# Woven attention: unscaled probabilities, and an output scaled by rows of inverses that pass through memory

## The chip, the cores and the metric

One Trainium2 chip, one of its cores. The metric is the time of one execution in device microseconds (us); smaller is better. The kernel before took 2072.51 us, the median of 3 runs (2071.71 to 2074.53).

## The reference, cut to what matters

A stack of layers on 512 tokens of width 1024, in float32. Three of the layers hold an attention, each followed by an output projection. Two have sinks (a window attention, a chunk band attention), the third has a bias from a table. In all three a softmax is divided by its row sum before it is multiplied with the values:

```python
m = jnp.maximum(jnp.max(scores, axis=-1, keepdims=True), sink_l)
p = jnp.exp(scores - m)
denom = jnp.sum(p, axis=-1, keepdims=True) + jnp.exp(sink_l - m)
p = (p / denom).astype(v.dtype)
out = jnp.einsum('bnkgqs,bnskd->bnqkgd', p, vb)
...
else:
    p = jax.nn.softmax(s, axis=-1)
o = jnp.einsum('bhgqj,bjhd->bqhgd', p.astype(v.dtype), v_c)
```

## The kernel before

Activations lie transposed: features on the 128 partitions, the 512 tokens in the free dimension. A weight matrix comes from memory in pairs of tiles (`raw`). ScalarE (ACT) rounds a piece to `w_hi` (L1621), VectorE (DVE) subtracts to get the rest `w_lo` (L1629), and TensorE (PE) makes each product of three matmuls of 128x512 (L1184 to L1186): hi by hi, hi by lo, lo by hi. One such triple is a *step*. The activations are split in the same way; for the attention's output the two halves are `mix_hi` and `mix_lo`, which the trace calls `act`.

An attention is woven into the steps of the projections around it: in1/out1 and in2/out2 (the grouped attentions, a = 0 and 1) and in3/out3 (the wide one). The work is cut into *slots*, and a table of step numbers (`GSLOTS`, `SLOTS`) says after which step each engine does its part of slot i. All engines run their instructions strictly in the order of the program, with semaphores between them. Two heads make a *chunk* c; there are 4 in a grouped attention and 8 in the wide one. A chunk has 4 blocks of 128 queries in 3 parts, one part to a slot: the unit u. A slot works on several units at once:

- PE, slot i: the scores of unit i (L504 wide, L666 grouped), the transposes of the probabilities of unit i-2 (L651, grouped alone), and the weighted sums of values of an older unit (L517, L684) into a bank of the accumulator (`pair_bank(c)`).
- DVE, slot i: for unit i-1 the inverse of the row sums (L572, L726) and the scaling of the probabilities, one instruction for each block and head (L576, L730); in the wide attention then a copy that splits each word in two halves (`halves`, L583); for unit i the biased maxima (L593, L740). After the last unit of a chunk the rest `mix_lo` (L599, L747).
- ACT, slot i: the exponentials of unit i with their row sums (L561, L715), the copy of the transposed unit out of the accumulator or out of `crossed` (L704, L549), and `mix_hi` of a finished chunk straight from the accumulator (L555, L708).
- SP, the queue that issues transfers: in the wide attention a transposing transfer of `halves` to `crossed` for each unit (L527); in the grouped ones the shifted rows of the rotary embedding (L760, L761) and the loads of weights (L1105).

Other DVE work stands between the slots in the same queue: `ring` (L2341, queries and keys of the wide attention, which PE's scores of a chunk wait for), `proj` (L2272) and the rotary embedding (L776 to L781) of the grouped ones, and the results of the output projection (`h` L2309, `y` L2305 and L2355). Fourteen steps before the end of in1 and in2 PE transposes the values (L1485); it waits there for the tile that L2272 writes.

The output projection takes chunks 4 to 7 in its first 32 steps in out1 and out2 (made by the pooling and by the recurrence) and the attention's own 0 to 3 after them, out3 the chunks 0 to 3 and then 4 to 7; out1's step 36 is the first that reads chunk 3 of the attention. DVE's slot 15, which ends that chunk, stands at step 35 of out1 and at step 32 of out2.

Of the kernel before, what the change touches and what calls it, by code (L numbers as in the profile page):

```python
# [5 lines left out]
F32 = mybir.dt.float32  # L6
# [6 lines left out]
P = 128  # L13
# [155 lines left out]
def build(nc, x_t, vecs, weights, mixer_consts, pool_tab, small_consts, pool_w, sinks, rel_bias, out_t, scratch, skew, stop=None):  # L169
# [4 lines left out]
    with ExitStack() as ctx:  # L174
# [51 lines left out]
        mask = mconst[:, 2 * T:2 * T + 384]  # L226
        squares = at("squares", [P, KD * T], F32, act_at)
# [103 lines left out]
        w_normed = sem("w_normed")  # L331
# [17 lines left out]
        g_normed = sem("g_normed")  # L349
# [32 lines left out]
        std4, inv4 = tiny[:, 112:116], tiny[:, 116:120]  # L382
        sink_col, neg_sink, decay = tiny[:, 80:96], tiny[:, 96:112], tiny[:, 128:192]
# [105 lines left out]
        def slot_pe(pe, i):  # L489
# [31 lines left out]
        def slot_sp(sp, u):  # L521
# [17 lines left out]
        def slot_act(eng, i):  # L539
# [12 lines left out]
            c, s = divmod(i - 7, NPARTS)  # L552
            if s == 0 and 0 <= c < KD:
                eng.wait_ge(w_weighed, NPARTS * (c + 1))
                eng.activation(chunk(mix_hi, c), pair_bank(c), ACT.Copy).then_inc(w_mix_hi, 1)  # L555
            if 0 <= i < STEPS:
                c, s, own, _ = blocks_of(i)
                for part, (n, at_, w) in enumerate(own):
                    for hh in range(2):
# [3 lines left out]
                                       accum_out=ROW[:, part_col(i, part, hh)]).then_inc(w_probs, 1)  # L563

        def slot_dve(eng, i, link):

            u = i - 1
            if 0 <= u < STEPS:
# [14 lines left out]
                eng.tensor_copy(to, words).then_inc(w_halved, 1)  # L583
            if 0 <= i < STEPS:
# [53 lines left out]
        def grouped_pe(pe, a, i):  # L638
# [31 lines left out]
            for u in (i - 4, i - 3) if i % 2 == 0 else ():  # L670
# [4 lines left out]
                if s == 0:  # L675
                    pe.wait_ge(g_v_done, a + 1)
                    if c >= 2:
                        pe.wait_ge(mix_ready, KD * a + 4 + c - 1)
# [15 lines left out]
        def grouped_act(eng, a, i):  # L694
# [10 lines left out]
            c = mixed_at(a, i)  # L705
            if c is not None:
                eng.wait_ge(g_weighed, u0 + len(GPARTS[a]) * (c + 1))
                eng.activation(chunk(mix_hi, c), pair_bank(c), ACT.Copy).then_inc(mix_hi_ready, 1)  # L708
            if 0 <= i < GSTEPS[a]:
                c, s, own, _ = grouped_blocks(a, i)  # L710
                for part, (n, lo, hi, at_, w) in enumerate(own):
                    for hh in range(2):
# [3 lines left out]
                                       accum_out=ROW[:, grouped_col(i, part, hh)]).then_inc(g_exped, 1)  # L716

        def grouped_dve(eng, a, i, link):
# [3 lines left out]
            if 0 <= u < GSTEPS[a]:  # L722
# [3 lines left out]
                link(eng.reciprocal(INV[:, grouped_col(u, n=rows)], ROW[:, grouped_col(u, n=rows)]))  # L726
                for part, (n, lo, hi, at_, w) in enumerate(own):
                    for hh in range(2):
                        p = exps_at(a, u, hh)[:, at_:at_ + w]
                        ins = eng.tensor_scalar(p, p, INV[:, grouped_col(u, part, hh)], None, ALU.mult)  # L730
# [344 lines left out]
        def _(sp):  # L1075
            for st in stages:
# [30 lines left out]
                if st.name in IN:  # L1107
                    a = IN.index(st.name)
                    out = OUTS[a]
                    for g in range(-2 * KD * 2, 2 * KD * (st.pairs + out.pairs - 2)):  # L1110
# [6 lines left out]
                        if g % KD == 1 and g // KD - 1 in ROPED[a]:  # L1117
                            rope_sp(sp, a, g // KD - 1)
# [1505 lines left out]
```

## Time and profile before

| what | value |
|---|---|
| median of 3 runs | 2072.51 us |
| the profiled execution | 2075.14 us, of which its span is 2073.3 us |
| granted clock of TensorE, mean | 0.999 |
| busy, share of the span: PE, DVE, ACT | 99%, 57%, 37% |

The span is the time from the first to the last instruction of the program in the profile; 1.8 us of the execution lie around it. PE is the engine that everything else must keep fed. Its matmuls overlap and their ends are modelled, so that lost time shows best in the distance of one matmul's start to the next: in a step it is 0.23 us.

### The profile page before, as it was taken

How to read it: one execution, taken by the hardware profiler on the slowest of the kernel's cores; microseconds unless marked ns; L12 is line 12 of the kernel's file. 1: busy time of each engine (PE TensorE's matmuls, PEld its weight loads, DVE VectorE, ACT ScalarE, POOL GpSimd, SP SyncE). 2: the span in 40 equal slices, each digit the busy share in tenths (PEclk: the TensorE clock that was granted, in tenths of full speed). 3: DMA queues.
4: the chain of work that ended last, by engine and by line, in shares of the span. 5: the costliest groups of instructions: out<-in, count | busy, mean ns of one | idle time of the engine just before them, and what ended most of it. 6: DMA issues, size and time to landing. Idle time of an engine off the chain costs nothing.

```text
span 2073.3 us, 27109 instructions
## 1 busy us (share of the span) xinstructions
PE 2055.2 (99%) x10366; PEld 1689.7 (81%) x10366; DVE 1180.8 (57%) x1927; ACT 759.5 (37%) x1163; POOL 123.8 (6%) x138
## 2 busy tenths in 40 slices
PE   9999999999999999999999999999999999999999
PEld 7888888778888888988788888888876688888887
DVE  5444433786444433487778666633668877666433
ACT  5222222354322222463454322222557753222222
POOL 0000000400000000000002000000413120000001
PEclk9999999999999999999999999999999999999999
DMA  8322233312222222331221322233347622232222
GB/s 255 121 98 101 76 99 108 130 47 96 86 101 101 96 69 98 116 102 62 92 82 62 101 101 101 76 99 109 103 128 166 158 78 102 101 101 95 72 96 82
DMA packets 78300, 210.90 MB, mean 102 GB/s; under 512 B 46192, under 2 KB 49568, under 8 KB 61840
## 3 DMA queue, kind: packets, MB, share of 16 engines
q1 hardware_dynamic: 72896, 184.04, 28.0%
q0 software_dynamic: 2992, 12.31, 2.1%
q10 hardware_dynamic: 2336, 13.52, 1.8%
q8 instruction: 49, 0.80, 0.2%
q14 instruction: 27, 0.22, 0.0%
HBM read 195.08 MB, written 7.38 MB: 98 GB/s over the span
## 4 chain that ended last, share of the span: by engine, by line
PE 88%; DVE 6%; ACT 3%; issue 1%; DMA 1%; POOL 0%; SPq 0%; ACTq 0%; DVEq 0%
PE ps L1184 28%; PE ps L1185 28%; PE ps L1186 28%; ACT weigh L561 2%; DVE w_lo L1629 1%; PE ps L684 1%; DVE weigh L576 1%; DVE halves L583 1%; PE ps L666 1%; ACT w_hi L1621 1%; PE ps L651 1%; DVE weigh L593 1%; DMA h<-in_x_t 0%; ACT x_split L1707 0%; PE ps L1171 0%
## 5 line engine op out<-in xcount | busy, mean ns | idle before, releaser
L1184 PE MATMUL ps<-x_split,w_hi 128*128 128x512 f32 (+1 forms) x1774 | 697.6, 393 | 1.2 <-DVE x_split L1667 1.2
L1186 PE MATMUL ps<-x_split,w_lo 128*128 128x512 f32 (+1 forms) x1774 | 688.3, 388 | 0.0
L1185 PE MATMUL ps<-x_split,w_hi 128*128 128x512 f32 (+1 forms) x1774 | 688.1, 388 | 0.0
L1611 ACT ACTIVATE w_hi<-raw 128x2048 fp32r<-128x2048 f32 (+3 forms) x144 | 242.2, 1682 | 495.2 <-PE ps L1186 492.3
L1184 PEld LDWEIGHTS ps<-x_split,w_hi 128*128 128x128 f32 x1774 | 333.3, 188 | 79.2 <-issue 12.5
L1639 DVE TENSOR_TENSOR w_lo<-raw,w_hi 128x2048 fp32r<-128x2048 f32 (+3 forms) x144 | 287.9, 1999 | 179.7 <-ACT w_hi L1611 179.2
L1186 PEld LDWEIGHTS ps<-x_split,w_lo 128*128 128x128 f32 x1774 | 333.2, 188 | 68.5
L1185 PEld LDWEIGHTS ps<-x_split,w_hi 128*128 128x128 f32 x1774 | 333.5, 188 | 66.5 <-issue 1.0
L1184 PE MATMUL ps<-act,w_hi 128*128 128x512 f32 (+1 forms) x1026 | 376.9, 367 | 3.4 <-DVE w_lo L1629 3.1
L1185 PE MATMUL ps<-act,w_hi 128*128 128x512 f32 (+1 forms) x1026 | 372.9, 363 | 0.0
L1186 PE MATMUL ps<-act,w_lo 128*128 128x512 f32 (+1 forms) x1026 | 372.7, 363 | 0.0
L1184 PEld LDWEIGHTS ps<-act,w_hi 128*128 128x128 f32 x1026 | 193.9, 189 | 39.8 <-DVE w_lo L1629 4.7
L1186 PEld LDWEIGHTS ps<-act,w_lo 128*128 128x128 f32 x1026 | 194.1, 189 | 30.3
L1185 PEld LDWEIGHTS ps<-act,w_hi 128*128 128x128 f32 x1026 | 194.2, 189 | 29.2
L1946 ACT ACTIVATE act<-prod 128x512 f32 (+1 forms) x88 | 55.6, 632 | 202.4 <-DVE prod L2415 202.4
L1629 DVE TENSOR_TENSOR w_lo<-raw,w_hi 128x512 fp32r<-128x512 f32 x140 | 101.0, 731 | 46.9 <-ACT w_hi L1621 46.6
L2395 DVE TENSOR_TENSOR gate<-ps,rstd 128x512 f32<-128x512 f32 x44 | 30.4, 692 | 170.2 <-PE ps L1186 170.1
L2439 DVE TENSOR_TENSOR act<-prod,act 128x512 f32 (+1 forms) x88 | 60.9, 693 | 88.3 <-ACT act L1946 88.3
L1621 ACT ACTIVATE w_hi<-raw 128x512 fp32r<-128x512 f32 x140 | 83.0, 619 | 57.0 <-PE ps L1186 54.0
L2398 DVE TENSOR_TENSOR shifted<-ps,rstd 128x512 f32<-128x512 f32 x44 | 30.4, 691 | 100.8 <-PE ps L1186 100.7
L1928 ACT ACTIVATE gated<-gate 128x512 f32<-128x512 f32 x88 | 54.8, 623 | 86.8 <-DVE gate L2410 80.4
L2507 POOL TENSOR_TENSOR h<-h,gate 128x256 f32<-128x256 f32 x29 | 24.8, 856 | 983.7 <-DVE gate L2061 983.6
(248 smaller groups left out, 1760.3 us busy)
## 6 DMA issues: line engine op xcount, KB each, us to landing
raw<-in_w_up SPq DMA_DIRECT2D x87, 1024.0 KB, 4.9
raw<-in_w_down SPq DMA_DIRECT2D x29, 768.0 KB, 4.2
raw<-in_w_in SPq DMA_DIRECT2D x20, 1024.0 KB, 4.9
raw<-in_w_down SPq DMA_DIRECT2D x29, 640.0 KB, 3.8
raw<-in_w_out SPq DMA_DIRECT2D x8, 1024.0 KB, 4.9
raw<-in_w_in ACTq DMA_DIRECT2D x8, 1024.0 KB, 5.5
skew<-scratch POOLq DMA_DIRECT2D x1, 5120.0 KB, 32.4
biases<-skew POOLq DMA_DIRECT2D x16, 256.0 KB, 4.3
```

The lines of the kernel that those rows point to most:

```text
L561: eng.activation(weigh_at(i, hh)[:, at_:at_ + w], weigh_at(i, hh)[:, at_:at_ + w], ACT.Exp, bias=NEG[:, part_col(i, part, hh)], scale=-1.0 ...
L1184: pe.matmul(own, hi, rhs_hi, start=start, stop=False)
L1185: pe.matmul(own, hi, rhs_lo, start=False, stop=False)
L1186: return pe.matmul(own, lo, rhs_hi, start=False, stop=stop)
L1611: eng.activation(w_hi[:, w], raw[:, w], ACT.Copy).then_inc(hi_rounded, 1)
L1621: eng.activation(w_hi[:, w], raw[:, w], ACT.Copy).then_inc(hi_piece, 1)
L1629: ins = eng.tensor_tensor(w_lo[:, w], raw[:, w], w_hi[:, w].bitcast(F32), ALU.subtract)
L1639: eng.tensor_tensor(w_lo[:, w], raw[:, w], w_hi[:, w].bitcast(F32), ALU.subtract).then_inc(lo_rounded, 1)
L1928: eng.activation(gated[:, :], gate[:, :], ACT.Silu if st.evac == "silu" else ACT.Gelu)\
L1946: eng.activation(chunk(act, f), prod[:, :], ACT.Copy).then_inc(prod_hi, 1)
L2395: eng.tensor_tensor(gate[:, :], bank(b), rstd[:, :], ALU.mult).then_inc(gate_ready, 1)
L2439: eng.tensor_tensor(chunk(act, KF + f), prod[:, :], chunk(act, f).bitcast(F32), ALU.subtract)\
```

## The change

In all three attentions the probabilities are no longer scaled. The exponentials go on as they are (PE's transposes and DVE's `halves` now wait for the exponentials themselves), and the inverses of the row sums are collected per chunk in 8 columns of a small tile (`OUT_INV`: 2 heads by 4 blocks, one query to a partition). The accumulated output has its queries in the free dimension, so it needs these inverses as rows. They get there through memory: when a chunk is complete, SP writes the 128x8 numbers to a small table `factors` in memory (`factors_out_sp`), one element at a time since neighbours in the table lie in different partitions, and reads two rows of 512 back, each repeated on 64 partitions (`factors_in_sp`, two transfers). DVE multiplies the accumulator's bank with them into `mix_raw`. ACT makes `mix_hi` from `mix_raw`, now behind its exponentials of the slot, and DVE makes `mix_lo` a slot later, for the last chunk at once. `mix_raw` lies where `mix_lo` does. The memset of `ssum` in out3 goes behind the first pass, and the transposes of the values stand 12 steps before the end of in1 and in2 instead of 14.

```diff
@@ the wide attention
-                    pe.wait_ge(w_mix, c - 1)
+                    pe.wait_ge(w_mixed, c - 1)
+        def inverses_of(c):
+            return OUT_INV[:, c % 2 * 2 * NB:(c % 2 + 1) * 2 * NB].rearrange("p (h n) -> p h n", n=NB)
+
+        def factors_out_sp(sp, c, inverted, mixed):
+
+            sp.wait_ge(*inverted)
+            if c >= 2:
+                sp.wait_ge(*mixed)
+            rows = factors[c % 2 * 2:c % 2 * 2 + 2, :].rearrange("h (n q) -> q h n", q=P)
+            sp.dma_start(rows, inverses_of(c), allow_slow_non_contiguous=True).then_inc(f_written, 16)
+
+        def factors_in_sp(sp, c, to, done):
+
+            sp.wait_ge(f_written, 16 * (done + c + 1))
+            for hh in range(2):
+                row = factors[c % 2 * 2 + hh:c % 2 * 2 + hh + 1, :]
+                sp.dma_start(to[c % 2][64 * hh:64 * hh + 64, :], row.to_broadcast([64, T])).then_inc(f_landed[c % 2], 16)
...
+            c, s = divmod(i - 7, NPARTS)
+            if s == 0 and 0 <= c < KD:
+                eng.wait_ge(w_mixed, c + 1)
+                eng.activation(chunk(mix_hi, c), chunk(mix_raw, c), ACT.Copy).then_inc(w_mix_hi, 1)
...
-                link(eng.reciprocal(INV[:, part_col(u, n=rows)], ROW[:, part_col(u, n=rows)]))
-                for part, (n, at_, n_keys) in enumerate(own):
-                    for hh in range(2):
-                        p = weigh_at(u, hh)[:, at_:at_ + n_keys]
-                        ins = eng.tensor_scalar(p, p, INV[:, part_col(u, part, hh)], None, ALU.mult)
-                ins.then_inc(w_normed, 1)
-                eng.wait_ge(w_normed, u + 1)
...
+                sums = ROW[:, part_col(u, n=rows)].rearrange("p (n h) -> p h n", h=2)
+                eng.reciprocal(inverses_of(c)[:, :, own[0][0]:own[0][0] + len(own)], sums).then_inc(w_inverted, 1)
...
             if s == 0 and 0 <= c < KD:
+                eng.wait_ge(w_weighed, NPARTS * (c + 1))
+                eng.wait_ge(f_landed[c % 2], 32 * ((KD + c) // 2 + 1))
+                eng.tensor_tensor(chunk(mix_raw, c), pair_bank(c), factor_rows[c % 2], ALU.mult).then_inc(w_mixed, 1)
+            if s == 1 and 0 <= c < KD or s == 0 and c == KD - 1:
                 eng.wait_ge(w_mix_hi, c + 1)
-                eng.tensor_tensor(chunk(mix_lo, c), pair_bank(c), chunk(mix_hi, c).bitcast(F32), ALU.subtract).then_inc(w_mix, 1)
+                eng.tensor_tensor(chunk(mix_lo, c), chunk(mix_raw, c), chunk(mix_hi, c).bitcast(F32), ALU.subtract).then_inc(w_mix, 1)
@@ the grouped attentions (their ACT part is moved as above)
-                pe.wait_ge(g_normed, u0 + u + 1)
+                pe.wait_ge(g_exped, grouped_rows(a, u) + 2 * len(own))
...
             if c is not None:
-                eng.wait_ge(mix_hi_ready, KD * a + 4 + c + 1)
-                eng.tensor_tensor(chunk(mix_lo, c), pair_bank(c), chunk(mix_hi, c).bitcast(F32), ALU.subtract).then_inc(mix_ready, 1)
+                eng.wait_ge(g_weighed, u0 + len(GPARTS[a]) * (c + 1))
+                eng.wait_ge(f_landed[c % 2], 32 * ((4 * a + c) // 2 + 1))
+                eng.tensor_tensor(chunk(mix_raw, c), pair_bank(c), g_factor_rows[c % 2], ALU.mult).then_inc(g_mixed, 1)
+            done = c if c == 3 else mixed_at(a, i - 1)
+            if done is not None and (done < 3 or c == 3):
+                eng.wait_ge(mix_hi_ready, KD * a + 4 + done + 1)
+                eng.tensor_tensor(chunk(mix_lo, done), chunk(mix_raw, done), chunk(mix_hi, done).bitcast(F32), ALU.subtract)\
+                    .then_inc(mix_ready, 1)
@@ SP, in1 and in2
+                            if slot_at(a, g - 1) == units:
+                                factors_out_sp(sp, c, (g_inverted, a * GSTEPS[0] + units), (g_mixed, 4 * a + c - 1))
+                            if slot_at(a, g - 5) == units:
+                                factors_in_sp(sp, c, g_factor_rows, 4 * a)
@@ SP, in3
                         slot_sp(sp, u)
+                        c, s = divmod(u, NPARTS)
+                        if s == 0 and c:
+                            factors_in_sp(sp, c - 1, factor_rows, KD)
+                        if s == NPARTS - 1:
+                            factors_out_sp(sp, c, (w_inverted, NPARTS * (c + 1)), (w_mixed, c - 1))
+                    factors_in_sp(sp, KD - 1, factor_rows, KD)
@@ PE and ACT, in1 and in2
-                    if g == end - 14:
+                    if g == end - 12:
```

On DVE one stretch of in3 read so before, from the inverse of a chunk's first unit to the maxima of its third (ISA is the maximum, `act` is `mix_lo`):

```order
L572 RECIPROCAL tiny<-tiny 128x4 [waits w_probs]
L576 TENSOR_SCALAR weigh<-weigh,tiny 128x128 [waits dve_step]
L576 TENSOR_SCALAR weigh<-weigh,tiny 128x128
L576 TENSOR_SCALAR weigh<-weigh,tiny 128x256 x2
L583 COPY halves<-weigh 128x1536 [waits w_crossed1,w_normed]
...
L599 TENSOR_TENSOR act<-ps,act 128x512 [waits w_mix_hi]
L1629 TENSOR_TENSOR w_lo<-raw,w_hi 128x512 [waits hi_piece] x2
L572 RECIPROCAL tiny<-tiny 128x2 [waits w_probs]
L576 TENSOR_SCALAR weigh<-weigh,tiny 128x384 [waits dve_step]
L576 TENSOR_SCALAR weigh<-weigh,tiny 128x384
L583 COPY halves<-weigh 128x1536 [waits w_crossed0,w_normed]
L593 ISA weigh,tiny<-ps,biases 128x512 [waits w_scores]
```

and now:

```order
L602 COPY halves<-weigh 128x1536 [waits w_crossed0,w_probs]
L606 RECIPROCAL tiny<-tiny 128x2x2 [waits f_written]
...
L623 TENSOR_TENSOR mix_raw<-ps,shifted 128x512 [waits f_landed0,w_weighed]
L1673 TENSOR_TENSOR w_lo<-raw,w_hi 128x512 [waits hi_piece] x2
L602 COPY halves<-weigh 128x1536 [waits w_crossed1,w_probs]
L606 RECIPROCAL tiny<-tiny 128x2
L616 ISA weigh,tiny<-ps,biases 128x512 [waits w_scores]
...
L626 TENSOR_TENSOR act<-mix_raw,act 128x512 [waits w_mix_hi]
```

The scalings are gone, the copy to `halves` comes first and the inverse behind it, the product stands where the rest stood, and the rest is behind the next unit's maxima.

At the end of out1's first pass, on DVE, before (the row of `h` that waits for `pair_done` is step 32, `act` is chunk 3's `mix_lo`):

```order
L2309 SCALAR_TENSOR_TENSOR h<-ps,h 128x512 [waits pair_done]
L1629 TENSOR_TENSOR w_lo<-raw,w_hi 128x512 [waits hi_piece]
L747 TENSOR_TENSOR act<-ps,act 128x512 [waits mix_hi_ready]
L2309 SCALAR_TENSOR_TENSOR h<-ps,h 128x512 [waits evacuated,part_done]
```

and now:

```order
L2353 SCALAR_TENSOR_TENSOR h<-ps,h 128x512 [waits pair_done]
L1673 TENSOR_TENSOR w_lo<-raw,w_hi 128x512 [waits hi_piece]
L774 TENSOR_TENSOR mix_raw<-ps,gated 128x512 [waits f_landed1,g_weighed]
L778 TENSOR_TENSOR act<-mix_raw,act 128x512 [waits mix_hi_ready]
L2353 SCALAR_TENSOR_TENSOR h<-ps,h 128x512 [waits evacuated,part_done]
```

Where one row took chunk 3 to its end, there are now two, with ACT's copy between them.

On PE around the transposes of the values in in1, before:

```order
L1186 MATMUL ps<-x_split,w_lo 128x512
L1485 MATMUL ps<-small,proj 128x128 [waits evacuated]
L1485 MATMUL ps<-small,proj 128x128 x3
```

and now, behind two more steps, with the next slot's transposes following a step later:

```order
L1230 MATMUL ps<-x_split,w_lo 128x512
L1529 MATMUL ps<-small,proj 128x128 [waits evacuated]
L1529 MATMUL ps<-small,proj 128x128 x3
L1228 MATMUL ps<-x_split,w_hi 128x512
L1229 MATMUL ps<-x_split,w_hi 128x512
L1230 MATMUL ps<-x_split,w_lo 128x512
L678 MATMUL ps<-small,g_exps_84 128x128 [waits g_copied,g_exped]
```

## Rows read from the trace of the kernel before

**Rows 1.** The page: packets of the transfers, and the chain by line.

```profile
DMA packets 78300, 210.90 MB, mean 102 GB/s; under 512 B 46192, under 2 KB 49568, under 8 KB 61840
...
PE ps L1184 28%; PE ps L1185 28%; PE ps L1186 28%; ACT weigh L561 2%; DVE w_lo L1629 1%; PE ps L684 1%; DVE weigh L576 1%; DVE halves L583 1%; PE ps L666 1%; ACT w_hi L1621 1%; PE ps L651 1%; DVE weigh L593 1%; DMA h<-in_x_t 0%; ACT x_split L1707 0%; PE ps L1171 0%
```

**Rows 2.** Windows, the wide attention: stretch; length, busy us by engine; clock, DMA.

```profile
1515.00:1680.00 165.00, 161.13 (x964) 116.86 (x964) 127.91 (x322) 111.46 (x234) 33.37 (x36) 0.99 0.62 150
```

**Rows 3.** Waits of PE in the wide attention: us in total, times, longest.

```profile
PE ps L1184 <- DVE w_lo L1629: 2.1, 1, 2.1
PE ps L504 <- DVE ring L2341: 1.6, 3, 0.6
```

**Rows 4.** The chain, 1652 to 1656 us: start, length, what.

```profile
1652.48 1.52 ACT weigh L561 x4
...
1654.56 0.70 DVE w_lo L1629
```

**Rows 5.** Windows, 1656 to 1660 us; the columns are those of Rows 2.

```profile
1656.00:1660.00 4.00, 4.00 (x15) 2.83 (x15) 3.42 (x6) 3.34 (x6) 0.00 (x0) 0.57 1.11 285
```

**Rows 6.** Groups of instructions: count, busy us, mean ns of one, idle before.

```profile
L576 DVE TENSOR_SCALAR weigh<-weigh,tiny 128x128 f32<-128x128 f32 (+3 forms) x64 | 22.8, 419 | 0.9
L730 DVE TENSOR_SCALAR g_exps<-g_exps,tiny 128x256 f32<-128x256 f32 (+2 forms) x64 | 19.6, 359 | 0.8
```

**Rows 7.** PE's timeline at the transposes of the values, in1 and in2.

```profile
425.30 0.66 PE L1485 MATMUL ps<-small,proj 128*128 128x128 f32 x4 [0.73 <-DVE proj L2272]
...
1014.29 0.66 PE L1485 MATMUL ps<-small,proj 128*128 128x128 f32 x4 [0.94 <-DVE proj L2272]
```

**Rows 8.** Who waited for `g_exps`: us in total, times.

```profile
  PEld ps L651: 0.8, 2
```

**Rows 9.** Timelines of DVE, ACT and PE, steps 32 to 36 of out1.

```profile
487.69 0.69 DVE L1629 TENSOR_TENSOR w_lo<-raw,w_hi 128x512 fp32r<-128x512 f32 x1
488.30 0.68 DVE L747 TENSOR_TENSOR act<-ps,act 128x512 fp32r<-128x512 f32 x1
...
487.56 0.58 ACT L708 ACTIVATE act<-ps 128x512 fp32r<-128x512 f32 x1
...
488.62 0.39 PE L1186 MATMUL ps<-act,w_lo 128*128 128x512 f32 x1
489.04 0.50 PE L1184 MATMUL ps<-act,w_hi 128*128 128x512 f32 x1
```

**Rows 10.** PE's timeline, the step behind slot 9 of in1.

```profile
465.48 0.50 PE L1184 MATMUL ps<-act,w_hi 128*128 128x512 f32 x1 [0.98 <-DVE w_lo L1629]
```

**Rows 11.** Timelines of DVE and PE, slots 12 to 15 of out2, and out1's slot 12.

```profile
476.87 0.16 DVE L726 RECIPROCAL tiny<-tiny 128x2 f32<-128x2 f32 x1
...
1057.52 0.15 DVE L726 RECIPROCAL tiny<-tiny 128x2 f32<-128x2 f32 x1
...
1065.37 0.68 DVE L1629 TENSOR_TENSOR w_lo<-raw,w_hi 128x512 fp32r<-128x512 f32 x1
...
1068.52 0.28 PE L1184 MATMUL ps<-act,w_hi 128*128 128x256 f32 x1
```

**Rows 12.** Issues of transfers: count, KB of one, median us to landing.

```profile
skew<-scratch POOLq DMA_DIRECT2D x1, 5120.0 KB, 32.4
...
out_t<-h SPq DMA_DIRECT2D x16, 128.0 KB, 1.8
...
g_swap<-proj ACTq DMA_DIRECT2D x4, 128.0 KB, 3.0
crossed<-halves SPq DMA_TRANSPOSE x24, 3.9
...
scratch<-shifted POOLq DMA_DIRECT2D x1, 24.0 KB, 4.4
```

**Rows 13.** Timelines of DVE and ACT, the last slots of out3.

```profile
1656.27 1.23 DVE L583 COPY halves<-weigh 128x2048 uint16<-128x2048 uint16 x1
...
1663.67 2.25 ACT L549 ACTIVATE turned<-crossed 128x1024 uint16<-128x1024 uint16 x2 [4.33 <-DMA crossed<-halves]
```

More of the change, by code:

```diff
@@ L166, in repeat, with build @@
         body(i)
-def build(nc, x_t, vecs, weights, mixer_consts, pool_tab, small_consts, pool_w, sinks, rel_bias, out_t, scratch, skew, stop=None):
+def build(nc, x_t, vecs, weights, mixer_consts, pool_tab, small_consts, pool_w, sinks, rel_bias, out_t, scratch, skew, factors, stop=None):
     names = [s.name for s in STAGES]
@@ L330, in build @@
         w_probs = sem("w_probs")
-        w_normed = sem("w_normed")
+        w_inverted = sem("w_inverted")
+        f_written = sem("f_written")
+        f_landed = [sem(f"f_landed{k}") for k in range(2)]
+        w_mixed = sem("w_mixed")
         w_halved = sem("w_halved")
@@ L348, in build @@
         g_exped = sem("g_exped")
-        g_normed = sem("g_normed")
+        g_inverted = sem("g_inverted")
+        g_mixed = sem("g_mixed")
         g_turned_ps = sem("g_turned_ps")
@@ L382, in build @@
         std4, inv4 = tiny[:, 112:116], tiny[:, 116:120]
+        OUT_INV = tiny[:, 48:64]
+        factor_rows = (shifted[:, 2:2 + T], ssum[:, :])
+        g_factor_rows = (shifted[:, 2:2 + T], gated[:, :])
         sink_col, neg_sink, decay = tiny[:, 80:96], tiny[:, 96:112], tiny[:, 128:192]
@@ L551, in slot_act @@
                 ins.then_inc(w_copied, 1)
[L552 to L555, printed above, removed]
             if 0 <= i < STEPS:
@@ L583, in slot_dve @@
                 eng.tensor_copy(to, words).then_inc(w_halved, 1)
+                if s == 0 and c >= 2:
+                    eng.wait_ge(f_written, 16 * (KD + c - 1))
+                sums = ROW[:, part_col(u, n=rows)].rearrange("p (n h) -> p h n", h=2)
+                eng.reciprocal(inverses_of(c)[:, :, own[0][0]:own[0][0] + len(own)], sums).then_inc(w_inverted, 1)
             if 0 <= i < STEPS:
@@ L677, in grouped_pe @@
                     if c >= 2:
[L678 removed]
+                        pe.wait_ge(g_mixed, 4 * a + c - 1)
                 to = 0
@@ L704, in grouped_act @@
                 eng.activation(g_turned_at(a, u)[:, :, 0:w], both[:, :, 0:w], ACT.Copy).then_inc(g_copied, 1)
[L705 to L708, printed above, removed]
             if 0 <= i < GSTEPS[a]:
@@ L716, in grouped_act @@
                                        accum_out=ROW[:, grouped_col(i, part, hh)]).then_inc(g_exped, 1)
+            c = mixed_at(a, i)
+            if c is not None:
+                eng.wait_ge(g_mixed, 4 * a + c + 1)
+                eng.activation(chunk(mix_hi, c), chunk(mix_raw, c), ACT.Copy).then_inc(mix_hi_ready, 1)
         def grouped_dve(eng, a, i, link):
@@ L725, in grouped_dve @@
                 eng.wait_ge(g_exped, grouped_rows(a, u) + rows)
[L726 to L730, printed above, removed]
-                ins.then_inc(g_normed, 1)
+                if s == 0 and c >= 2:
+                    eng.wait_ge(f_written, 16 * (4 * a + c - 1))
+                blocks = slice(own[0][0], own[-1][0] + 1, max(1, own[-1][0] - own[0][0]))
+                sums = ROW[:, grouped_col(u, n=rows)].rearrange("p (n h) -> p h n", h=2)
+                eng.reciprocal(inverses_of(c)[:, :, blocks], sums).then_inc(g_inverted, 1)
             if 0 <= i < GSTEPS[a]:
@@ L1118, in _ @@
                             rope_sp(sp, a, g // KD - 1)
+                        for c in range(4):
+                            units = len(GPARTS[a]) * (c + 1)
+                            if slot_at(a, g - 1) == units:
+                                factors_out_sp(sp, c, (g_inverted, a * GSTEPS[0] + units), (g_mixed, 4 * a + c - 1))
+                            if slot_at(a, g - 5) == units:
+                                factors_in_sp(sp, c, g_factor_rows, 4 * a)
                 elif st.name in OUT:
@@ L1848, in _ @@
                             key_swap_act(eng, a)
-                        if g == end - 14:
+                        if g == end - 12:
                             eng.wait_ge(g_v_ps, a + 1)
@@ L2347, in _ @@
                 if st.name == "out3":
-                    link(eng.memset(ssum[:, :], 0.0))
                     for g in range(1, KD * KD // 2 + 1):
@@ L2356, in _ @@
                         rest_piece(eng, pieces_at(IN3, OUT3, IN3_STEPS + g - 2))
+                    link(eng.memset(ssum[:, :], 0.0))
                     break_out_dve(st, BARRIERS[st.name])
```

4 lines of the change are left out of this document (3 added, 1 removed).

## The prediction

> **What bounds the kernel.** I read the page first. PE is busy for 99% of the span, and its three lines of products are 84% of the chain [rows 1], so only what makes PE wait counts, and what DVE and ACT save is worth nothing elsewhere. The windows say how little there is to win: in the 165 us of the wide attention PE is busy for 161, while DVE has 128 and ACT 111 [rows 2]. All of DVE's scaling, 22.8 and 19.6 us [rows 6], is eight times what PE is found to lose below. Next I read the waits of PE in that stretch. There are two: the scores of a chunk wait three times for `ring`, 1.6 us together, and one step waits 2.1 us for `w_lo` [rows 3]. The chain says why the second is late: exponentials on ACT for 1.52 us, then the rounding, then DVE's `w_lo` at 1654.56 [rows 4]. DVE and ACT hand the work to and fro in each slot (maximum, exponentials, `w_hi`, `w_lo`, then inverse, scaling, `halves`, and the next maximum), and this loop, not the sum of either's work, takes about as long as PE's slots: three waits of some 0.5 us at chunks of 17 us. Behind the long wait the granted clock is 0.57 in the mean of 1656 to 1660 us [rows 5]: full speed is 2.4 GHz, so PE stood at 1.2 GHz for (1 - 0.57) / 0.5 x 4.0 = 3.4 us and lost half of that, 1.7 us.
>
> **What is removed, wide attention.** 64 scalings, 22.8 us, or 2.85 us of a chunk's loop of 17. In exchange the loop takes in ACT's copy to `mix_hi`, 0.58 us [rows 9], which stood ahead of the exponentials while ACT waited and now stands between them and the rounding. The product of 0.68 us (priced by the subtraction from the same bank, of the same shape) runs beside the exponentials, and so does `mix_lo` a slot later. Net: the loop is 2.3 us shorter per chunk, four times the 0.5 us that it was late. I take all of the `ring` waits, 1.6 us, as gone. At the end the slots come 4 steps apart instead of 5.33 and the loop falls behind again, but it starts from no delay instead of some 3 us, and must be 2.1 us earlier: I take the wait for `w_lo`, 2.1 us, and with it the low clock, 1.7 us. Together **5.4 us**.
>
> **What is removed, grouped attentions.** 64 scalings, 19.6 us. Their waits are few. PE waits for the values' tile, 0.73 us in in1 and 0.94 us in in2 [rows 7]. The transposes move two steps back, 6 x 0.23 = 1.4 us, past both waits, and DVE, which is late there with scalings and rotary work ahead of the tile, is earlier too: **1.7 us**. PE's transposes now start at the exponentials without DVE between: the weight loads of these transposes waited 0.8 us in all [rows 8], part of it beside matmuls that still ran, and I take 0.3 us. The wait of 0.98 us at slot 9 of in1 [rows 10] stays: `w_lo` is there behind four maxima, which themselves wait for PE, and behind the rest, and the product that takes the rest's place costs the same.
>
> **What is added on the path.** The end of a chunk was ACT, then DVE; it is DVE, ACT, DVE. In the middle of an attention nobody waits for it. At the ends:
> - out1, step 35 [rows 9]: DVE ends `w_lo` at 488.30, the rest starts at once, and PE starts at 489.04, 0.2 us later than its rhythm (488.62 + 0.23). Now the product takes the slot of 488.30, ACT's copy can start when it ends, 488.99, and ends at 489.57 plus some 0.05 us, the rest ends at 490.30: PE is 1.3 us later than before. A **loss of 1.3 us**. Nothing covers it, since the step behind reads that chunk.
> - out2: the slot stands at step 32, and its DVE is free from 1065.97. Product, copy, rest: done at 1068.1; the second pass starts at 1068.52 and reads the chunk 1.1 us later [rows 11]. Hidden, with 1.5 us to spare. out3 is built alike, and its memset of `ssum`, 0.5 us, lies beside PE's first half tile.
>
> **The way through memory.** For each chunk: one write of 1,024 single elements and two reads of 512-element rows to 64 partitions. No row shows such a write. From below: the output's transfers to memory land in 1.8 us. From above: the transfer of 2,048 rows of 2.5 KB lands in 32.4 us, and half as many pieces at its pace take 16 us. The nearest rows are `crossed`, 3.9 us though nearly all of the 46,192 packets under 512 bytes [rows 1] must be those of its 24 transfers, up to 1,925 each, and the small transfer to memory, 4.4 us; I take 4.4. The reads are like `g_swap`, 3.0 us, with 0.6 us of SP's issue for each of a pair [rows 12], so 4.0 us. The whole way: **8.4 us** behind the last inverse of a chunk. In the middle it has three slots or more. At the ends: in out2 the inverse is at 1057.52 and DVE wants the row at 1066.0, PE at 1067.5, so 9.8 us; in out1 476.87 to 488.30, 11.3 us [rows 11, 9]. In out3 the last write queues behind the unit's transposing transfer, which here landed so late that ACT waited 4.3 us, since a load of weights shared the engines [rows 13]: `halves` 1656.27, `turned` 1663.67. With DVE 3 to 4 us earlier, I find the row just in time or up to 1 us late: a loss of **0.5 us**. What waits behind it: DVE's product blocks `y` and `w_lo`, SP's wait for the write blocks its next transposing transfers, which have a slack of about 5 us.
>
> The Trainium skill speaks against this write ("DMA: Bandwidth & Descriptors", Rules for kernel authors): a last dimension that is not contiguous becomes one descriptor for each element and should be rearranged, and its Specifications say that under 512 bytes an element is read, modified and written. The packets of `crossed` are under 512 bytes as well, and its transfers land in 3.9 us, and no row here shows a write of 4 bytes to memory, so the trace neither confirms nor refutes the rule at this size; by it the second rival below would be the likelier one.
>
> **Sum.** 5.4 + 1.7 + 0.3 - 1.3 - 0.5 = 5.6 us less. The profiled execution took 2075.14 us (span 2073.3, 1.8 around it) and would take 2069.5; it was 2.6 us above the median of 2072.51, so I predict **2066.9 us**.
>
> **Rivals.**
> - *The loop stays as long.* If ACT, which now has the copy behind its exponentials, or the two `w_lo` in a row set the pace, half of the 5.4 us stays: 2069.6 us. For it: ACT's 0.58 us is certain. Against: it needs four times that to fill the gap.
> - *The rows come late (slower than before).* One mechanism: the write takes longer than 4.4 us. From a way of 9.8 us on, each further us costs one in out2, from about 9.1 in out3 (with the clock's 1.7 us again, once PE waits over 2 us) and from 11.3 in out1. At a write of 9 us the way is 13 us: 3.2 + 3.9 + 1.7 + 1.7 = 10.5 us of new waits, 5.4 + 1.7 + 0.3 - 1.3 = 6.1 us won: 2076.9 us, the point where it is slower by 0.2%. It decides from a write of 8 us on. For it: single elements, memory as the target. Against: `crossed` and the 4.4 us of the small transfer.
> - *out1 and out3 lose nothing*, because DVE is ahead there and the chain of three is hidden: the fixed order speaks against it. With the 1.3 and 0.5 us not lost, and up to 0.6 us of waits too short for these rows: 2064.5 us.
> - *Somewhat late.* A write of 5.5 to 8 us eats most of the gain: 2069 to 2074 us.
>
> **Chances.** Forecast 0.48, hidden and better 0.08, loop stays 0.12, somewhat late 0.18, late and slower 0.14. A measurement of this kernel tells 0.2%, 4.1 us, from no change: the line for faster is 2068.4, for slower 2076.7. Most of the forecast's own cases (0.45) and the better one are faster, with a third of the loop's: 0.57 faster. Same: 0.30. Slower: 0.13. The range from 2063.5 to 2075.0 us leaves out the worst of the late cases and little else; the forecast's own range is 2064.5 to 2068.8.
>
> **What would show it.** DVE's busy time falls by 22.8 + 19.6 - 16 x 0.68 = 31.5 us. In the wide attention PE waits for neither `ring` nor `w_lo`, and its clock stays at 1.00. The transposes of the values follow their step at once. In out1 PE waits some 1.5 us for the new `mix_lo`. The write lands 4 to 5 us after its issue, and in out2 and out3 PE does not wait for `mix_lo`. I am wrong if the write lands later than 6 us after its issue, or if the loop is still at DVE's or ACT's pace.

## The result and the profile of the changed kernel

The changed kernel takes 2118.14 us (median of 6 runs, 2111.55 to 2119.38) against 2073.41 us before (6 runs on the same chip, 2071.71 to 2074.53). The ratio is 1.0209, 95% interval 1.0194 to 1.0225: 2.1% slower. Forecast were 2066.9 us and a range that ended at 2075.0. The profiled execution took 2113.35 us, its span is 2111.6 us.

The page of the changed kernel, busy time, transfers and chain; its packets and chain answer to [rows 1]:

```profile
PE 2069.2 (98%) x10366; PEld 1700.2 (81%) x10366; DVE 1146.3 (54%) x1815; ACT 761.5 (36%) x1163; POOL 123.8 (6%) x138
...
DMA packets 97500, 215.16 MB, mean 102 GB/s; under 512 B 63344, under 2 KB 66720, under 8 KB 81040
...
PE 86%; DMA 8%; DVE 2%; POOL 2%; ACT 1%; SPq 1%; issue 0%; DVEq 0%; POOLq 0%
PE ps L1228 28%; PE ps L1230 27%; PE ps L1229 27%; DMA biases<-skew 4%; DMA factors<-tiny 2%; POOL biases L433 1%; PE ps L693 1%; DMA gated<-factors 1%; PE ps L678 1%; DMA crossed<-halves 0%; PE ps L711 0%; DVE w_lo L1673 0%; SPq L535 0%; POOL biases L435 0%; PE ps L1205 0%
```

DVE's work did what it was meant to: 1180.8 us before, 1146.3 now. But transfers, which carried nothing worth naming in the chain of [rows 1], are 8% of the chain that ended last. Half of that is `biases<-skew`, the loads of the bias tiles that DVE's maximum reads in the wide attention, issued by GpSimd (POOL). What waits for transfers? The waits in the wide attention, 1515 to 1750 us, of PE, DVE and SP's queue (engine, line, what ended the wait: us in total, times, longest); before, PE had 2.1 and 1.6 us [rows 3]:

```profile
PE ps L525 <- ACT turned L575: 8.0, 3, 4.3
PE ps L1228 <- DVE act L626: 4.5, 1, 4.5
PE ps L1228 <- DVE y L2398: 3.9, 1, 3.9
PE ps L512 <- DVE ring L2385: 3.8, 3, 2.5
...
DVE halves L602 <- DMA crossed<-halves: 22.4, 10, 4.3
DVE weigh L616 <- POOL biases L435: 11.8, 5, 3.4
...
DVE mix_raw L623 <- DMA ssum<-factors: 6.1, 1, 6.1
...
SPq L554 <- DMA factors<-tiny: 56.2, 7, 9.7
```

Only one of PE's waits is for a scaled chunk (4.5 us, for the last one, whose row DVE got 6.1 us late). The others follow waits of DVE and ACT for two other kinds of transfer: for `crossed`, for which DVE waits ten times, and for the biases, for which it waits five times. PE's wait of 3.9 us for `y` comes behind one of each, 4.3 us for `crossed` and then 3.4 us for the biases. POOL's own waits, 1515 to 1750 us, before and then now:

```profile
POOL biases L425 <- DMA biases<-skew: 52.6, 12, 6.9
POOL biases L423 <- DVE tiny L593: 44.3, 6, 31.2
...
POOL biases L433 <- DMA biases<-skew: 88.5, 12, 11.0
```

Before, POOL waited six times until DVE had freed a tile, so it had time to spare. Now it waits so once, at the start, and then only for its loads.

The page's issues (count, KB of one, median us to landing) show that transfers became slow which the change does not touch; before, these three had 4.3, 5.8 and 3.9 us:

```profile
biases<-skew POOLq DMA_DIRECT2D x16, 256.0 KB, 5.5
raw<-in_w_out ACTq DMA_DIRECT2D x4, 1024.0 KB, 7.8
...
crossed<-halves SPq DMA_TRANSPOSE x24, 8.5
factors<-tiny SPq DMA_DIRECT2D x16, 4.0 KB
```

One chunk of the wide attention, timelines of SP's queue and then of ACT:

```profile
1590.70 0.53 SPq L547 DMA_DIRECT2D factors<-tiny  x1
1592.77 1.45 SPq L535 DMA_TRANSPOSE crossed<-halves  x1
1603.42 1.09 SPq L554 DMA_DIRECT2D shifted<-factors  x2
...
1603.79 1.76 ACT L575 ACTIVATE turned<-crossed 128x768 uint16<-128x768 uint16 x2 [4.28 <-DMA crossed<-halves]
```

The write is issued at 1590.70 and SP, which waits for it, goes on at 1603.42: 12.7 us for 4 KB. The transposing transfer issued 2 us behind it lands with the write, just before ACT's copy at 1603.79, 11.0 us after its issue, where 3.9 us was usual. The 16 writes take 8.1 to 14.5 us from issue to the last increment of their semaphore. Their packets are sent within some 2 us of the issue in twelve of them, in the other four, in the wide attention, within 2.5 to 5 us. What takes the rest of the time is the confirmation.

Six places where PE turns the root of a norm (L1178 before, L1222 after), as their starts stand in PE's timelines, divide the loss; us from the span's start:

```
              before    after   without the way through memory
in in1        376.75    376.08    376.14
in up2        527.49    530.62    527.03
in in2        894.94    898.08    894.49
in up3       1120.27   1133.66   1118.58
in in3       1490.75   1504.14   1489.09
in up4       1722.98   1761.24   1715.48
```

Against before, the stretch from in1 to up2 is 3.8 us longer, that from in2 to up3 10.2, and that from in3 to up4 24.9. The third column is from the first experiment below.

### The profile page after: what moved, and what is told of

Same layout as the page of the kernel before. It is cut to its first block, busy times and chain, and to the rows that moved or that the text cites. A ratio compares the mean times of both kernels' runs of the same rounds, so it can differ in the third digit from the quotient of the medians.

```text
span 2111.6 us, 27075 instructions
## 1 busy us (share of the span) xinstructions
PE 2069.2 (98%) x10366; PEld 1700.2 (81%) x10366; DVE 1146.3 (54%) x1815; ACT 761.5 (36%) x1163; POOL 123.8 (6%) x138
## 4 chain that ended last, share of the span: by engine, by line
PE 86%; DMA 8%; DVE 2%; POOL 2%; ACT 1%; SPq 1%; issue 0%; DVEq 0%; POOLq 0%
PE ps L1228 28%; PE ps L1230 27%; PE ps L1229 27%; DMA biases<-skew 4%; DMA factors<-tiny 2%; POOL biases L433 1%; PE ps L693 1%; DMA gated<-factors 1%; PE ps L678 1%; DMA crossed<-halves 0%; PE ps L711 0%; DVE w_lo L1673 0%; SPq L535 0%; POOL biases L435 0%; PE ps L1205 0%
## 5 line engine op out<-in xcount | busy, mean ns | idle before, releaser
L1228 PEld LDWEIGHTS ps<-act,w_hi 128*128 128x128 f32 x1026 | 197.2, 192 | 58.7 <-DVE act L778 7.9
L1229 PEld LDWEIGHTS ps<-act,w_hi 128*128 128x128 f32 x1026 | 197.4, 192 | 29.6
L2551 POOL TENSOR_TENSOR h<-h,gate 128x256 f32<-128x256 f32 x29 | 24.9, 858 | 997.7 <-DVE gate L2105 997.6
```

Source lines behind the costliest of these rows:

```text
L1228: pe.matmul(own, hi, rhs_hi, start=start, stop=False)
L1229: pe.matmul(own, hi, rhs_lo, start=False, stop=False)
```

## Experiments

**Without the way through memory (`no_way`).** Write, reads and their waits are gone; the product takes the tile `rstd` in place of the rows.

```
-                            if slot_at(a, g - 1) == units:
-                                factors_out_sp(sp, c, (g_inverted, a * GSTEPS[0] + units), (g_mixed, 4 * a + c - 1))
-                            if slot_at(a, g - 5) == units:
-                                factors_in_sp(sp, c, g_factor_rows, 4 * a)
...
-                eng.wait_ge(f_landed[c % 2], 32 * ((KD + c) // 2 + 1))
-                eng.tensor_tensor(chunk(mix_raw, c), pair_bank(c), factor_rows[c % 2], ALU.mult).then_inc(w_mixed, 1)
+                eng.tensor_tensor(chunk(mix_raw, c), pair_bank(c), rstd[:, :], ALU.mult).then_inc(w_mixed, 1)
```

> The changed kernel without the write and the reads of the inverses and without the waits for them; the attention's output is multiplied by another tile of the same shape, so the output is not the reference's. Theory A (the way through memory costs all that is lost): the terms of the prediction without the way remain, 6.1 us less than before, 2066 to 2069 us. Rival C (the new order on DVE and ACT costs by itself, the chain of product, copy and rest above all): 2080 us or more, with PE waiting for the rest of a chunk in the middle of the wide attention. In out1 PE waits some 1.3 us for the last chunk by both.

Measured: 2067.38 us, ratio 0.9971 (0.9961 to 0.9982). Theory A holds and rival C falls: all that is lost, and more, is in the way through memory. In this run PE waits nowhere in the wide attention for `ring` or `w_lo` and its clock stays at full speed there. In out1 it waits, as forecast, for the last chunk's rest (timeline of PE):

```profile
488.58 0.50 PE L1217 MATMUL ps<-act,w_hi 128*128 128x512 f32 x1 [1.41 <-DVE act L772]
```

**One run for each partition (`whole_runs`).** The same 4 KB in 128 pieces of 32 bytes.

```
-            rows = factors[c % 2 * 2:c % 2 * 2 + 2, :].rearrange("h (n q) -> q h n", q=P)
+            rows = factors[c % 2 * 2:c % 2 * 2 + 2, :].rearrange("h (q j) -> (h q) j", j=2 * NB)
```

> The changed kernel with one thing different: each partition writes its 8 inverses as one run of 32 bytes, 128 pieces instead of 1,024; the reads are the same, so the rows hold the inverses in a wrong order and the output is scaled by wrong queries' inverses. Theory A (the single elements make the write late): it lands in 3 to 4 us, SP waits for it at most 4 us, and the time is 2066 to 2071 us, as in the run without the way or up to 2 us above. Theory D (any way through memory is this slow, write and confirmation): it still lands in 8 us or more and the time stays above 2100 us.

Measured: 2067.23 us, ratio 0.9971 (0.9959 to 0.9982); issues of this run:

```profile
crossed<-halves SPq DMA_TRANSPOSE x24, 4.2
...
factors<-tiny SPq DMA_DIRECT2D x16, 4.0 KB, 1.9
```

The write lands in 1.9 us and costs nothing, nor do the reads. Theory D falls: it is the form of the write, not memory.

**Transfers alone (`alone`, `alone2`).** Two programs with nothing but transfers, on an idle chip.

> This program computes nothing of the reference: it issues transfers one at a time on an idle chip and waits for each, four times each. The same write as in the changed kernel (1,024 elements of 4 bytes to two rows of memory), half of it and 128 elements of it, the same elements 64 bytes apart, the 4 KB in 128 runs of 32 bytes, 16 KB in 128 rows of 128 bytes, 4 KB in 8 rows of 512 bytes, one read of a row to 64 partitions, a transposing transfer of 128 x 1,024 halves, and the write with a transposing transfer issued right behind it, on the same queue and on another. In the changed kernel the pieces of a write are sent within 2 us of the issue, but its semaphore comes 8 to 14 us after it. Theory A (the write itself is slow to be confirmed): the write lands in 8 to 10 us alone too. Theory B (it is only slowed by the other transfers of the kernel): 4 to 5 us alone. Within A, if the number of pieces sets it: the half lands in 5 to 6 us, the far elements as late as the near ones, 8 to 10 us. If pieces of one 64-byte line disturb each other: the far elements land in 3 to 4 us. The runs of 32 bytes: 2 to 3 us in any case. If a slow write holds what is behind it on its queue, the transposing transfer behind it lands in 9 us or more and the one from another queue in 4; if not, both in 4 to 5 us.

SP's queue in `alone`: start, length from the first issue to the end of the fourth's. Since SP waits for each, (length - 0.4) / 3 is the time of one (for a transposing transfer, whose issue takes 1.3 us, (length - 1.3) / 3).

```profile
9.43 31.71 SPq L36 DMA_DIRECT2D near<-tiny  x4
54.04 29.97 SPq L39 DMA_DIRECT2D single<-tiny  x4
95.38 26.76 SPq L42 DMA_DIRECT2D quarter<-tiny  x4
130.83 9.29 SPq L45 DMA_DIRECT2D far<-tiny  x4
142.31 4.56 SPq L48 DMA_DIRECT2D runs<-tiny  x4
147.94 4.57 SPq L51 DMA_DIRECT2D turned_rows<-tiny  x4
...
170.18 10.50 SPq L60 DMA_TRANSPOSE crossed<-halves  x4
182.50 0.41 SPq L63 DMA_DIRECT2D after_near<-tiny  x1
182.95 1.29 SPq L64 DMA_TRANSPOSE crossed<-halves  x1
194.64 0.39 SPq L63 DMA_DIRECT2D after_near<-tiny  x1
...
230.53 36.96 SPq L69 DMA_TRANSPOSE crossed<-halves  x4
```

The kernel's write (`near`) takes 10.4 us alone, so theory B falls: no other traffic is needed. Half of it (`single`) takes 9.9 us and 128 elements (`quarter`) 8.8, so the number of pieces hardly matters, while the same 1,024 pieces 64 bytes apart (`far`) take 3.0. In this, theory A's second form holds (pieces close together disturb each other). Runs of 32 bytes take 1.4. A transposing transfer takes 3.1 us alone and lands with the write when it is issued behind it (the pair takes 12.1 us), and also when the write goes out on ACT's queue in the same moment (11.9 each), where 4 us was expected.

> A second program of single transfers on an idle chip, four times each, which computes nothing of the reference. The run before it showed that 1,024 elements next to each other land in 9.4 to 13.2 us, 128 elements still in 7.5 to 9.8, and 1,024 elements 64 bytes apart in 2.5 to 3.2. Theory G (pieces that share 64 bytes of memory wait for each other, and 16 of them share it in the kernel's write): one line of 16 elements from 16 partitions lands in 3 us or more against 1.4 for pieces that share nothing; elements 8 bytes apart (8 share a line) land in 5 to 7 us, 32 bytes apart (2 share it) in 3 to 4. Theory H (any write of 4 bytes beside another, by the number of pieces): 8 and 32 bytes apart land alike, in 8 us or more. A line of 64 bytes that one partition fills with 16 single elements tells whether it matters that the pieces come from different partitions: 3 us or less if it does, over 8 if not. A plain load of 1 MB, 8 KB to each partition, behind the kernel's write on the same queue or beside it from another: 4.5 to 5 us if only transposing transfers are held, 10 us or more if all are; the load alone 4.5 to 5 us.

```profile
8.78 6.60 SPq L37 DMA_DIRECT2D line<-tiny  x4
18.12 14.20 SPq L40 DMA_DIRECT2D pairs<-tiny  x4
36.59 9.62 SPq L43 DMA_DIRECT2D pairs<-tiny  x4
49.08 41.69 SPq L46 DMA_DIRECT2D own_line<-tiny  x4
```

The time falls with the number of pieces in the same 64 bytes: 16 of them 10.4 us, 8 (8 bytes apart, L40) 4.6 us, 2 (32 bytes apart, L43) 3.1 us, 1 3.0 us. Theory G's gradation holds, H falls. But G's price for one line alone, 3 us or more, does not: a single line of 16 elements took 1.3 to 3.0 us, where `quarter`, eight such lines, took 8.8. The 128 lines which one partition each fills with 16 single elements (L46, 2,048 pieces) took 13.8 us, so it does not matter whether the pieces come from different partitions. And plain loads are held too (issues of this run):

```profile
plain<-in_x_t SPq DMA_DIRECT2D x4, 1024.0 KB, 5.1
held<-in_x_t SPq DMA_DIRECT2D x4, 1024.0 KB, 15.2
apart<-in_x_t ACTq DMA_DIRECT2D x4, 1024.0 KB, 11.8
```

The load that takes 5.1 us alone takes 15.2 behind the write on its queue and 11.8 beside it from another.

**The far elements in the kernel (`far_apart`).**

```
+    far = nc.dram_tensor("far", (4, T, 16), F32).ap()
...
-            rows = factors[c % 2 * 2:c % 2 * 2 + 2, :].rearrange("h (n q) -> q h n", q=P)
+            rows = far[c % 2 * 2:c % 2 * 2 + 2, :, 0:1].rearrange("h (n q) o -> q h (n o)", q=P)
...
-                row = factors[c % 2 * 2 + hh:c % 2 * 2 + hh + 1, :]
+                row = x_t[hh:hh + 1, 0:T]
```

> The changed kernel with the same number of single elements written, 1,024 of 4 bytes, but each 64 bytes from the next; the reads take rows of the input x instead, so the output is not the reference's. If pieces that share 64 bytes of memory are the cause, the write lands in 2.5 to 4 us and the time is that of the run with runs of 32 bytes, 2067 to 2069 us. If the number of pieces of 4 bytes is the cause inside the kernel, where other transfers run, it stays above 2090 us.

Measured: 2067.33 us, ratio 0.9970 (0.9958 to 0.9981).

```profile
crossed<-halves SPq DMA_TRANSPOSE x24, 3.9
...
far<-tiny SPq DMA_DIRECT2D x16, 4.0 KB, 3.0
```

As many pieces of 4 bytes as in the changed kernel, and none of its loss. That settles that the write is slow by how close its pieces lie in memory, and not by their number. How large the stretch of memory is that they must not share is not settled: alone, pieces 32 bytes apart were as quick as those 64 bytes apart (3.1 and 3.0 us). The spread pieces also cover more memory, 64 KB in place of 4, and no run separates the two.

**The reads one unit later (`read_later`).** Nothing of the computation is left out.

```
-                        if s == 0 and c:
+                        if s == 1 and c:
                             factors_in_sp(sp, c - 1, factor_rows, KD)
```

> The changed kernel, complete, with one thing different: in the wide attention SP issues a chunk's reads, and stands in the wait for its write, one unit later, behind the next transposing transfer instead of in front of it. Theory E (what costs most in the middle of the wide attention is SP, which stands in that wait of up to 9.7 us while transposing transfers are due): the waits of PE between 1590 and 1700 us, 23 us with some 10 us of low clock, fall by half or more, and the time is 2090 to 2100 us; the ends of the attentions stay late. Theory F (transposing transfers are late because the write's pieces and confirmations hold their queue): under 5 us are gained, 2113 to 2118 us.

Measured: 2137.24 us, ratio 1.0309 (1.0289 to 1.0330), slower than the changed kernel. Theory E falls. F is right that freeing SP gains nothing, but its 2113 to 2118 us was missed as well: this costs 19 us more. The waits of DVE and ACT in this run, 1515 to 1750 us:

```profile
DVE halves L602 <- DMA crossed<-halves: 49.4, 10, 8.8
...
ACT turned L575 <- DMA crossed<-halves: 59.8, 11, 9.5
```

In the changed kernel SP's wait kept all but one transposing transfer of a chunk out of the write's time. Here SP issues two of them into it (timeline of its queue):

```profile
1585.51 0.59 SPq L547 DMA_DIRECT2D factors<-tiny  x1
1586.20 6.51 SPq L535 DMA_TRANSPOSE crossed<-halves  x2
1597.67 1.62 SPq L554 DMA_DIRECT2D ssum<-factors  x2
```

**The write alone (`write_only`).** The write as it is; no reads, nobody waits for a row, SP does not wait for the write just issued; the product takes `rstd`.

```
+            if done + c >= 2:
+                sp.wait_ge(f_written[c % 2], 16 * ((done + c) // 2))
             rows = factors[c % 2 * 2:c % 2 * 2 + 2, :].rearrange("h (n q) -> q h n", q=P)
```

> The changed kernel with the write of single elements as it is and without the reads; nothing waits for the rows (the output is scaled by another tile), and SP no longer stands in the wait for a write, it only sees that the write of two chunks ago has landed. Theory A1 (most of the loss in the wide attention is that the transposing transfers are held by the write, wherever SP waits): PE loses 20 us or more between 1580 and 1700 us, transposing transfers land in 8 us or more, the grouped attentions lose nothing, and the time is 2085 to 2100 us. Theory A2 (the loss is that the rows and what SP issues behind its wait are late): 2067 to 2070 us, as in the run without the way through memory.

Measured: 2103.09 us, ratio 1.0141 (1.0124 to 1.0157): theory A1, 3 us above its band; A2 falls. By the marks of the table above its in3 and out3 take 30.7 us longer than before, 36.5 longer than without the way, and its in1 to out2 lose nothing. PE's longest waits there (1515 to 1750 us) are for `crossed` at one remove:

```profile
PE ps L525 <- ACT turned L577: 15.1, 6, 7.8
PE ps L512 <- DVE ring L2383: 7.6, 2, 7.2
```

DVE waits 44.2 us for `crossed` there and 6.9 us for the biases. So in the wide attention the write alone is enough for a loss of this size, by holding other transfers; how the loss divides between `crossed` and the biases, no run separates. In the grouped attentions nothing is lost when nobody waits for a row, so their loss is that the rows come late: in the changed kernel DVE waits 12.6 us for them there.

**The shift alone (`shift_only`).** The kernel before with `if g == end - 12:` for `end - 14` on PE and ACT.

> The kernel before with one part of the change: the transposes of the values two steps later in in1 and in2. The prediction gave this part, together with DVE being earlier there, 0.73 + 0.94 us; in the run without the way through memory both waits are gone. If the shift alone does it, both waits are gone here too and the middle of the program is 1.6 us earlier; if DVE's freedom from the scalings was needed, a wait of 0.3 us or more stays at one of the two. Nothing else differs from before: about 1.6 us less than before in the same stretches of the trace, which a time alone can't tell from no change.

Both waits for the values' tile are gone, and by the marks in1 with out1 is 1.0 us shorter and in2 with out2 0.6 us, 1.6 in all, as the shift alone was to give (0.73 and 0.94). In in2 PE now waits 0.6 us for DVE's maxima instead. The time of its one execution, 2072.91 us, tells nothing at this size.

**Turned on DVE (`turned`).** Nothing of the computation is left out. DVE turns the tile with the inverses in blocks of 32 x 32, so that a partition holds 32 queries of one inverse, and each writes one row of 128 bytes.

```
+            eng.transpose(f_tile(c), tiny[:, 32:64]).then_inc(f_turns, 1)
...
-            rows = factors[c % 2 * 2:c % 2 * 2 + 2, :].rearrange("h (n q) -> q h n", q=P)
-            sp.dma_start(rows, inverses_of(c), allow_slow_non_contiguous=True).then_inc(f_written, 16)
+            rows = factors[c % 2 * 32:(c % 2 + 1) * 32, :].rearrange("j (g i) -> g j i", i=32)
+            sp.dma_start(rows, f_tile(c)).then_inc(f_written, 16)
...
-                row = factors[c % 2 * 2 + hh:c % 2 * 2 + hh + 1, :]
+                at_ = c % 2 * 32 + 16 + c % 2 * 2 * NB + hh * NB
+                row = factors[at_:at_ + NB, :].rearrange("(o n) q -> o (n q)", o=1)
```

> A complete version: DVE turns the 128 x 32 tile that holds the inverses (blocks of 32 x 32) once for each chunk, some 0.1 to 0.2 us, and the write takes 128 rows of 128 bytes to memory; the reads take the rows of the chunk as before. Alone such a write landed in 1.4 us. Expected: the write lands in 1.4 to 2.5 us, PE waits nowhere for a row, and the time is that of the run without the way, 2067 to 2069 us, 0.3% below the kernel before. If the turning itself, 16 more instructions on DVE between inverses and maxima, puts the loop of the wide attention back on the path, 2070 to 2073 us.

Measured: 2067.28 us, ratio 0.9971 (0.9959 to 0.9982), faster than before, by 0.3%, and than the changed kernel. The last increment that the trace has of the write's semaphore comes 2.0 to 2.4 us after the issue. The window of the wide attention, 165 us long as in [rows 2] and 1 us earlier (same columns):

```profile
1514.00:1679.00 165.00, 164.99 (x1020) 121.72 (x1018) 118.21 (x285) 116.01 (x240) 32.62 (x36) 1.00 0.68 168
```

The group of the turning (count, busy us, mean ns, idle before):

```profile
L548 DVE STREAM_TRANSPOSE f_turned<-tiny 128x32 f32<-128x32 f32 x16 | 3.4, 212 | 1.3
```

PE is busy for all 165 us, where it had 161 before, and the 3.4 us of turning are hidden.

**Out1's last slot two steps earlier (`turned_early`).** This is `turned` with slot 15 of the first grouped attention at 55 instead of 57.

> The complete version with the turned inverses, and the last slot of the grouped attention of out1 two steps earlier (55 for 57 in its table), so that product, copy and rest of the last chunk end before the step that reads them. In the version without this PE waits 1.4 us there for the rest, the term that the prediction had as 1.3 us. If the wait is only the fixed order of the three, it is gone and the time is 1.4 us less than the turned version's, 2065.9 us; if the slot's own inputs are then late (its row, or the weighed values on PE), a wait of 0.5 us or more stays at another place.

Measured: 2066.75 us, ratio 0.9969 (0.9956 to 0.9981). The wait in out1 falls from 1.4 to 0.7 us and the marks show in1 with out1 0.8 us shorter: half of the term was order, the rest is still there. The 1.4 us of the expectation did not come; the 0.5 us in the times are less than runs differ.

## Why the prediction was wrong

- **The write: the step that failed.** "The nearest rows are `crossed`, 3.9 us ... and the small transfer to memory, 4.4 us; I take 4.4." It measured 8.1 to 14.5 us. The value was taken by analogy from transfers with pieces under 512 bytes. But the pieces of `crossed` are 256 bytes each (in `alone`, 256 KB in 1,024 packets) and go to 128 partitions; those of the write are 4 bytes, 16 of them into the same 64 bytes of memory. The runs show that lying this close is what makes them slow: 1,024 such pieces 64 bytes apart land in 3.0 us.
- **The way's budget.** "In the middle it has three slots or more" and "a slack of about 5 us" for the transposing transfers. Both were reckoned at 8.4 us. With a slow write the row was late in in2's middle as well: SP could issue the reads only from 1046.56 on, behind a write of 9.7 us, and they landed just before 1055.17, some 8 us later, with the next chunk's write issued beside them at 1049.23 (timelines of SP's queue and of DVE).

```profile
1046.56 2.57 SPq L554 DMA_DIRECT2D gated<-factors  x2
1049.23 0.53 SPq L547 DMA_DIRECT2D factors<-tiny  x1
...
1055.17 0.69 DVE L774 TENSOR_TENSOR mix_raw<-ps,gated 128x512 f32<-128x512 f32 x1 [5.25 <-DMA gated<-factors]
```

- **What a slow write costs: the second step that failed.** The rival "The rows come late" had the sign and the threshold (8 us), and 10.5 us of new waits at 9 us. It priced only those who wait for the row. Against the run without the way, the changed kernel loses 3.7 us in in1 and out1, 11.5 in in2 and out2, and 30.7 in in3 and out3, by the places in the first table (45.9 us together; the medians differ by 50.8, since the profiled execution was one of the quicker). For the last, the largest part, nobody need wait for a row at all: the write alone makes 36.5 us there. The text spoke of the queue behind SP's wait, never of transfers already issued, nor of those of other queues, as the biases' loads.
- **The rule weighed.** The Trainium skill ("DMA: Bandwidth & Descriptors", Rules for kernel authors) advises against a last dimension that is not contiguous, since it becomes one descriptor for each element. The advice was right here. Its ground, the number of descriptors, is not what cost most: as many far elements land in 3.0 us. The prediction put the rule aside because the trace had no such write; a wide bound (1.8 to 16 us) stood in the text, and the value was taken near its lower end.
- **Terms that held**, read in `no_way`: 5.8 us in the wide attention (5.4 forecast), the waits for `ring` and `w_lo` and the low clock gone; the shift 1.6 us (1.7); out1's chain 1.4 us lost (1.3); DVE's busy time down by 31.4 us there, to 1149.4, and by 34.5 in the changed kernel (31.5). Their sum without the way was 6.1 us, 2067.3 from 2073.4; measured 2067.38. The 0.5 us for out3 is not there once the write is quick. The 0.3 us for the start at the exponentials can't be told apart in these runs.
- "The loop stays as long" did not happen: PE waits for neither `ring` nor `w_lo` in the wide attention of `no_way`.
- **Clock.** Where PE stood for about 4 us its granted clock fell, as it had behind the wait of 2.1 us before [rows 5]. Behind the wait of 3.9 us for `y`, the window 1666 to 1677 us of the changed kernel has PE at 0.69 in the mean (length, busy; clock, DMA share, GB/s): (1 - 0.69) / 0.5 x 11 = 6.8 us at 1.2 GHz, 3.4 us on top of the wait. The rival reckoned 1.7 for such a place, "once PE waits over 2 us". That line did not hold: the clock fell behind a wait of 1.99 us (0.66 in the mean of 1614 to 1619 us) and stayed at full speed behind one of 2.48 us at 1622.61 (1.00 from 1619 to 1632 us). From 1515 to 1740 us the clock is 0.95 in the mean; by this it costs some 0.05 x 225 = 11 us (an estimate), and with PE's new waits of 20.8 us (8.0 + 4.5 + 3.9 + 3.8 + 0.6) that is about the 30.7 us of in3 and out3. The rival had reckoned with one such place.

```profile
1666.00:1677.00 11.00, 7.08 (x26) 0.69 1.13 173
```

## What to carry to other kernels

Scatter no single elements next to each other into memory: turn the tile first, so that each piece is a run of 32 bytes or more, or place the elements 32 or 64 bytes apart. When a new transfer is priced, count what is in flight beside it on any queue and not only who waits for it. And when a price has no row, forecast the case at both bounds with all its consequences before choosing the value; here one short program of single transfers would have measured it.

## What the runs showed of the hardware

- Elements of 4 bytes written to memory from SBUF, 1,024 in one transfer on an idle chip: 10.4 us with 16 in the same 64 bytes, 4.6 with 8, 3.1 with 2, 3.0 with 1. With 16, 512 pieces take 9.9 us and 128 still 8.8, but 16 pieces, one line, 1.3 to 3.0. Runs of 32 bytes and 128 rows of 128 bytes take 1.4. The packets of the 1,024 are sent within 1.6 us; the rest is confirmation. The Trainium skill ("DMA: Bandwidth & Descriptors", Anatomy of one DMA) lays most of a transfer's fixed 2 us, for transfers issued from GpSimd, to the receipt of the write. The 1.4 us of the runs and the 3.0 of the far elements are of that size; 10.4 us is five times it.
- Such a write holds transfers beside it, transposing ones (3.1 us alone, 12 beside it) and plain loads (5.1 us alone, 15.2 behind it, 11.8 from another queue). Why a few pieces in one line do this to the engines' other work stays open; no run here looked into them.
- DVE's turning of a 128 x 32 tile of 4-byte elements took 212 ns.
